# Narrow products of the norms' sums, router joins and rank columns widened to 96 moving columns

## The reference

```python
def ec_moe(h, w_router, w_gate, w_up, w_down):
    cap = EC_CAPACITY_FACTOR * n // N_EXPERTS
    aff = jax.nn.softmax(h.astype(jnp.float32) @ w_router.astype(jnp.float32), axis=-1)
    g, idx = lax.top_k(aff.swapaxes(1, 2), cap)
    xs = jax.vmap(lambda hb, ib: hb[ib])(h, idx)
    a = jax.nn.silu(jnp.einsum('becd,edf->becf', xs, w_gate)) * jnp.einsum('becd,edf->becf', xs, w_up)
    y = jnp.einsum('becf,efd->becd', a, w_down) * g[..., None].astype(h.dtype)
```

## Time and profile before

| | |
|---|---|
| median of 3 runs | 2208.03 us (2206.87 to 2209.65) |
| the profiled execution | 2207.79 us |
| its span | 2206.0 us |
| TensorE busy | 2164.8 us, 98% of the span |
| VectorE busy | 998.0 us, 45% |
| ScalarE busy | 375.3 us, 17% |
| mean granted clock of TensorE | 0.991 |
| DMA | 570.28 MB, mean 259 GB/s |

### The profile page before, as it was taken

The page is one execution under the profiler, slowest core; times in us unless marked ns, Lnnn a source line. Parts: engine busy times, 40 slices in busy tenths (PEclk is TensorE's granted clock), DMA queues, the critical chain, the costliest instruction groups (busy, mean ns, idle before and its releaser), DMA issues.

```text
span 2206.0 us, 25276 instructions
## 1 busy us (share of the span) xinstructions
PE 2164.8 (98%) x10282; PEld 1320.1 (60%) x10282; DVE 998.0 (45%) x1468; ACT 375.3 (17%) x743; POOL 78.8 (4%) x103
## 2 busy tenths in 40 slices
PE   7999999999999999999999999999999999999999
PEld 3443588888886777857444444437888744444443
DVE  2983397788845544832312222215555322222222
ACT  3003312002123112842100000002000300000000
POOL 1110100000021000001000000001000000000000
PEclk9999999999999999998999999999999899999999
DMA  9538244677641112032899999997112599999997
GB/s 348 193 97 297 77 153 153 234 257 282 212 179 39 39 53 77 1 153 115 367 428 429 428 430 428 428 426 261 68 77 81 242 411 428 428 429 429 428 429 310
DMA packets 110140, 570.28 MB, mean 259 GB/s; under 512 B 9929, under 2 KB 18670, under 8 KB 82414
## 3 DMA queue, kind: packets, MB, share of 16 engines
q1 hardware_dynamic: 107328, 564.55, 63.7%
q10 hardware_dynamic: 2734, 4.64, 0.9%
HBM read 561.06 MB, written 2.10 MB: 255 GB/s over the span
## 4 chain that ended last, share of the span: by engine, by line
PE 85%; DMA 9%; DVE 3%; ACT 1%; issue 1%; ACTq 0%; SPq 0%; POOL 0%; DVEq 0%
PE psum L1709 23%; PE psum L2210 18%; PE psum L2194 9%; PE psum L1440 6%; DMA ring<-in_moe_w_down_dram 5%; PE psum L2302 4%; PE psum L1857 4%; PE psum L2248 4%; PE psum L1881 3%; PE psum L2038 2%; DMA ring<-in_mlp_w_dram 2%; PE psum L2014 2%; PE psum L1989 2%; PE psum L1653 1%; DVE arena L2549 1%; PE psum L1603 1%
## 5 line engine op out<-in xcount | busy, mean ns | idle before, releaser
L2210 PE MATMUL psum<-ring,arena 128*64 128x512 f32 x2048 | 446.0, 594 | 3.6 <-DMA ring<-in_moe_w_up_dram 3.6
L2210 PEld LDWEIGHTS psum<-ring,arena 128*64 128x64 f32 x2048 | 144.3, 137 | 296.6 <-issue 284.7
L2194 PE MATMUL psum<-ring,arena 128*64 128x512 f32 x768 | 224.3, 594 | 1.7 <-DMA ring<-in_moe_w_down_dram 1.7
L3121 DVE TENSOR_TENSOR arena<-psum,arena 128x512 f32<-128x512 f32 x32 | 34.0, 1062 | 357.7 <-PE psum L2210 357.7
L1440 PE MATMUL psum<-hT,ring 128*128 128x512 f32 x416 | 181.9, 598 | 3.0 <-ACT hT L960 3.0
L1709 PE MATMUL psum<-ring 128*128 128x256 f32 x640 | 143.2, 380 | 3.4 <-DVE roots L2693 3.2
L1440 PEld LDWEIGHTS psum<-hT,ring 128*128 128x128 f32 x416 | 79.1, 191 | 103.1 <-issue 97.5
L1709 PE MATMUL psum<-hT,ring 128*128 128x256 f32 x608 | 135.9, 379 | 0.0
L1709 PEld LDWEIGHTS psum<-ring 128*128 128x128 f32 x640 | 120.9, 190 | 23.9 <-issue 7.8
L2248 PEld LDWEIGHTS psum<-arena 128*128 128x128 f32 x1024 | 118.4, 194 | 11.4 <-issue 11.4
L1709 PEld LDWEIGHTS psum<-hT,ring 128*128 128x128 f32 x608 | 115.3, 190 | 16.4 <-issue 0.8
(11 more groups left out here) (430 smaller groups left out, 2571.0 us busy)
## 6 DMA issues: line engine op xcount, KB each, us to landing
ring<-in_moe_w_gate_dram SPq DMA_DIRECT2D x64, 2048.0 KB, 19.0
ring<-in_moe_w_up_dram SPq DMA_DIRECT2D x64, 2048.0 KB, 16.1
ring<-in_moe_w_down_dram SPq DMA_DIRECT2D x44, 2048.0 KB, 18.9
ring<-in_ada_w_dram SPq DMA_DIRECT2D x24, 2048.0 KB, 8.1
ring<-in_mlp_w_dram SPq DMA_DIRECT2D x16, 2048.0 KB, 8.6
hT<-in_moe_w_down_dram SPq DMA_DIRECT2D x16, 2048.0 KB, 13.9
ring<-in_w_mod_dram SPq DMA_DIRECT2D x12, 2048.0 KB, 13.7
ring<-in_conv_w_in_dram SPq DMA_DIRECT2D x6, 2048.0 KB, 18.7
```

The costliest lines, as they stand in the source:

```text
L2194: ins = pe.matmul(psum[64 * e:64 * e + 64, bank + nh, :], src[:, 4 * h + k, 64 * e:64 * e + 64], w[:, k, nh * N:(nh + 1) * N], start=h == ...
L2210: ins = pe.matmul(psum[64 * nh:64 * nh + 64, bank + e, :], src[:, 4 * h + k, 64 * e:64 * e + 64], w[:, k, nh * N:(nh + 1) * N], start=h == ...
```

## The change

`COPIES = 96`. A view `copies(bank)` splits the first 4 x 96 columns of a bank into one run of 96 columns for each token group. Every narrow product now writes 96 columns: token sums and rank columns 96 times the same sum, joins six copies of the 16 logits, the x norm's sums 48 copies of the pair (and 48 columns with a stride of two where only one of the pair is made). The moving side is a wider slice of `ones_d`, or the old operand broadcast. Readers take the first copy. The rank columns of the second expert are written into bank 7 instead of bank 6. Number and order of the instructions and all waits stay as they were.

```diff
+        COPIES = 96
+        def copies(bank):
+            return psum[:, bank, 0:NT * COPIES].rearrange("p (t c) -> p t c", t=NT)
 ...
-                    ins = pe.matmul(psum[:, STAT, tt:tt + 1], src[:, tt * P:(tt + 1) * P], const("ones_d")[:, 0:1],
+                    ins = pe.matmul(copies(STAT)[:, tt, :], src[:, tt * P:(tt + 1) * P], const("ones_d")[:, 0:COPIES],
 ...
-                    at = psum[:, t % 6, tt * E:(tt + 1) * E]
+                    at = copies(t % 6)[:, tt, :].rearrange("p (c e) -> p c e", e=E)
+                    wide = [P, COPIES // E, E]
 ...
-                        ins = pe.matmul(at, tmp[:, 0, tt * P:(tt + 1) * P], const("stack")[:, 0:E], start=tt == 0,
+                        ins = pe.matmul(at, tmp[:, 0, tt * P:(tt + 1) * P],
+                                        const("stack")[:, 0:E].unsqueeze(1).to_broadcast(wide), start=tt == 0,
 ...
-                            ins = pe.matmul(at, xT[:, j, tt * P:(tt + 1) * P], rw_gain[:, layer, j, :],
+                            ins = pe.matmul(at, xT[:, j, tt * P:(tt + 1) * P],
+                                            rw_gain[:, layer, j, :].unsqueeze(1).to_broadcast(wide), ...
 ...
-                        ins = pe.matmul(at[:, w:w + 1], src[:, tt * P:(tt + 1) * P], const("ones_d")[:, 0:1],
+                        ins = pe.matmul(at[:, :, w], src[:, tt * P:(tt + 1) * P], const("ones_d")[:, 0:COPIES // 2],
 ...
-                        ins = pe.matmul(at, src[:, P * m:P * m + P], feature_w[:, tile, :], start=False, stop=last,
+                        ins = pe.matmul(at, src[:, P * m:P * m + P],
+                                        feature_w[:, tile, :].unsqueeze(1).to_broadcast([P, COPIES // 2, 2]), ...
 ...
-                            ins = pe.matmul(psum[:, BANK_WIDE[0], 2 * j + e:2 * j + e + 1], beats[e][m][:, P * j:P * j + P],
-                                            one[:, 0:1], start=m == j, stop=m == NT - 1, skip_group_check=True)
+                            ins = pe.matmul(copies(BANK_WIDE[e])[:, j, :], beats[e][m][:, P * j:P * j + P],
+                                            one[:, 0:1].to_broadcast([P, COPIES]), start=m == j, stop=m == NT - 1, skip_group_check=True)
 ...
-                        ins = pe.matmul(psum[:, STAT, at:at + 1], late_out[m][:, H * i + P * tt:H * i + P * tt + P],
-                                        const("ones_d")[:, 0:1], start=False, stop=True, skip_group_check=True)
+                        ins = pe.matmul(copies(STAT)[:, at, :], late_out[m][:, H * i + P * tt:H * i + P * tt + P],
+                                        const("ones_d")[:, 0:COPIES], start=False, stop=True, skip_group_check=True)
```

More of the change, by code:

```diff
@@ L945, in token_root @@
                     act.wait_ge(S["n_ms"], 1)
-                act.activation(n_tok[:, 0, :], psum[:, STAT, 0:NT], ACT.Sqrt, bias=eps[:, 0:1])\
+                act.activation(n_tok[:, 0, :], copies(STAT)[:, :, 0], ACT.Sqrt, bias=eps[:, 0:1])\
                     .then_inc(S["rms_ready"], 1)
@@ L1325, in softmax @@
                     act.wait_ge(S["sq_used"], DT * FFN0 + DT)
-                act.activation(tok[:, 0, :], psum[:, STAT, 0:NT], ACT.Sqrt, bias=eps[:, 0:1]).then_inc(S["rms_ready"], 1)
+                act.activation(tok[:, 0, :], copies(STAT)[:, :, 0], ACT.Sqrt, bias=eps[:, 0:1]).then_inc(S["rms_ready"], 1)
                 act.activation(tok[:, 2, 0:1], one[:, 0:1], ACT.Exp)
@@ L1551, in join_logits @@
                         for j in (() if layer and tt < 2 else (4, 5) if layer else (DT - 1,)):
-                            ins = pe.matmul(at, xT[:, j, tt * P:(tt + 1) * P], rw_gain[:, layer, j, :],
-                                            start=False, stop=j != 4, skip_group_check=True)
+                            ins = pe.matmul(at, xT[:, j, tt * P:(tt + 1) * P],
+                                            rw_gain[:, layer, j, :].unsqueeze(1).to_broadcast(wide), start=False, stop=j != 4, skip_group_check=True)
                 if part:
@@ L1559, in x_stat @@
                 for m, tt in enumerate(tts):
-                    at = psum[:, STAT, 2 * tt:2 * tt + 2]
+                    at = copies(STAT)[:, tt, :].rearrange("p (c w) -> p c w", w=2)
                     if tile is None:
-                        ins = pe.matmul(at[:, w:w + 1], src[:, tt * P:(tt + 1) * P], const("ones_d")[:, 0:1],
+                        ins = pe.matmul(at[:, :, w], src[:, tt * P:(tt + 1) * P], const("ones_d")[:, 0:COPIES // 2],
                                         start=w == 0 and m == 0, stop=False, skip_group_check=True)
                     else:
-                        ins = pe.matmul(at, src[:, P * m:P * m + P], feature_w[:, tile, :], start=False, stop=last,
+                        ins = pe.matmul(at, src[:, P * m:P * m + P],
+                                        feature_w[:, tile, :].unsqueeze(1).to_broadcast([P, COPIES // 2, 2]), start=False, stop=last,
                                         skip_group_check=True)
@@ L2775, in _ @@
                     w2_outputs(half, nh)
-            means = psum[:, STAT, 0:2 * NT].rearrange("p (t c) -> p c t", c=2)
+            means = copies(STAT)[:, :, 0:2].rearrange("p t c -> p c t")
             dve.wait_ge(S["x_ms"], 1)
@@ L3034, in wide @@
                     return ap.unsqueeze(2).to_broadcast([P, NT, E])
-                ps = psum[:, T_LG[layer] % 6, 0:NT * E].rearrange("p (a b) -> p a b", a=NT)
+                ps = copies(T_LG[layer] % 6)[:, :, 0:E]
                 dve.wait_ge(S["rms_ready"], ROUTED[layer] + 1)
@@ L3063, in route_all @@
                 link(dve.tensor_tensor(first_two, first_two,
-                                       psum[:, BANK_WIDE[0], 0:2 * NT].rearrange("p (t e) -> p t e", e=2), ALU.subtract))
+                                       psum[:, BANK_WIDE[0]:BANK_WIDE[1] + 1, 0:NT * COPIES]
+                                       .rearrange("p e (t c) -> p t e c", t=NT)[:, :, :, 0], ALU.subtract))
             def rounds(layer, rs):
```

## The result

The change makes the kernel faster: median 2197.95 us (2196.58 to 2200.86) against 2209.03 us (2206.87 to 2211.44), six runs each, a ratio of 0.995 with a 95% interval of 0.9939 to 0.9961. That is 11.1 us less, where 13 were forecast; 2197.95 lies just inside the forecast's own range of 2192 to 2198, at its upper end. The profiled execution took 2198.42 us with a span of 2196.6, against 2207.79 and 2206.0: 9.4 us less.

What follows compares the result with a forecast made beforehand. TensorE, slowed by 34.1 us at half clock, was taken to bound the kernel. Savings of 7.0 (layer 0), 5.0 (layer 1) and 1.0 (x norm), minus 0.1 for wider products, made 12.9 us: 2195 us, range 2192 to 2198.

Steps and rivals of the forecast that it cites:

- What sets the end, and the clock: TensorE sets the end nearly everywhere; its half-level clock, 34.1 us in both routes and x norm, would become full.
- Columns up to 128 are free: In the 248 widened records, spacing follows the clock alone, so 96 columns add only 0.1 us in all.
- Rival 4: Widened records: moving columns and weight loads don't overlap, 21 us added against 12.9 gained, 2216 us; chance 0.05.
- rival 2: Routes and x norm: copies don't feed the clock, stretches stay at 0.50, time about 2208 us; chance 0.07.
- Rival 3: Routes: transposes don't count as activity for the clock, so only 5.4 us is gained, 2202.4 us; chance 0.04.
- Layer 0, 7.0 us: Layer 0's route: with the full clock, the gather's second half starts at 1037.7 instead of 1044.66, saving 7.0 us.
- the affine turn: Layer 0's route: 32 small records, 1.39 us at half level, taken as between 0.7 and 1.39 at full.
- Layer 1, 5.0 us: Layer 1's route: the gather starts at 1730.05 instead of 1735.04, with waits of 0.9 and 0.45 us; 5.0 us saved.
- x norm, 1.0 us: The x norm's widening: eight records at full level end 0.8 to 1.0 us earlier; 1.0 us saved.
- Nothing is given back in the expert loops: Expert loops: an earlier gather frees ring slots earlier, so the DMA-bound stretch moves as a whole and all savings count.
- The sum: Whole kernel: 7.0 + 5.0 + 1.0 - 0.1 = 12.9 us saved, giving about 2195 us.
- Rival 1: Routes: the clock still falls in part at TensorE's new waits, giving 3.3 to 6.5 us back; chance 0.12.

Runs made afterwards that it cites:

- e1: The change's layout with the old 1, 2 and 16 moving columns, against the kernel before: median 2208.08 us against 2209.38, ratio 0.9997.
- e3: The change with only the rank columns put back to one column, against the kernel before: median 2202.21 us, ratio 0.9976.
- e2: The new layout with only the rank columns 96 wide, the other sums narrow, against the kernel before: median 2201.86 us, ratio 0.9973.
- e6: The change with 128 copies in place of 96: median 2197.99 us beside 2197.31 for the change on the same chip.

## Why the prediction was right, point by point

**What sets the end, and the clock.** Right. The half level stood where the narrow products were, and e1 to e3 move it with them. One of the forecast's two rows for a level that holds was luck, though: from 1506.4 to 1513.2 of the kernel before, one-column sums among spare products kept 1.00, but in e1 and e2 the same sums among the same spare products were followed by the half level, from 1512.7 and 1510.4. That mixture holds the level in some executions only. The gather of 128-column records was the sound half of the argument.

**Columns up to 128 are free.** Right, taken at 0.1 us. The median distance between starts is 0.112 us at full level with 1 column (L1467 before), 96 (L2125 after) and 128 (L2125 in e6). Rival 4 is refuted by e6, rival 2 by the first seven rows after and by e1.

**Transposes.** The Trainium skill says in "TensorE: Matmul & The Clock Gate", "Part 4: PE-mode transpose", that the full level does not engage for transposes; by that rule their stretches would have stayed at half level. The rows after, 1.00 from 1020.1 to 1030.3 with 24 transposes and the 8 of the widening in it, disagree, as the earlier trace rows did. Rival 3 is refuted.

**Layer 0, 7.0 us.** From the projections' end (L1521, now L1526, at 1018.22 and 1020.17) to the second half of the gather it is 20.08 us where it was 26.44: 6.4 us. The mis-sized term is the affine turn, put at 0.7 to 1.39 us, with the widening at a middle value. It took 1.38 us (1026.20 to 1027.58), as at half level, so the widening came 0.3 us later than forecast. Small excesses between the widening and the ranks (2.79 us, 2.7 forecast) and between the ranks and the first gather (5.80, 5.65 forecast) make most of the other 0.3 us. The wait ahead of the ranks was forecast as 0.5 and is 0.39; the one ahead of the gather, 0.25 in the forecast (1033.4 to 1033.65), is 0.23.

**Layer 1, 5.0 us.** From L1531 (1714.64, now L1536 at 1710.27) to the gather 15.61 us where it was 20.40: 4.8 us. Forecast waits 0.9 and 0.45, measured 0.87 and 0.39.

**x norm, 1.0 us.** 0.9 us.

**Nothing is given back in the expert loops.** Right: layer 0's gate products start 4.41 us earlier than before (1048.33 and 1043.92), and layer 1's joins behind the loops 4.31 us earlier (1717.88 and 1713.57). The last 460 us keep it as well: 9.2 us at layer 1's gate products (1742.74 and 1733.55), 9.4 at the end.

**The sum.** 6.4 + 4.8 + 0.9 = 12.1 us in the three places, 12.9 forecast. The step that a profile of before could not give is what happened outside them: in the execution profiled after, x norm's sums began 1.8 us later than before (674.56, 672.73), most of it around the half level from 190.6 (TensorE is 0.4 us ahead of the execution before at 191 and 1.0 us behind at 193; from there to the x norm's sums another 0.8 us was lost outside any fall), and another 1.0 us was lost between the x norm and the projections, where the fall at 869.9 is. 12.1 - 1.8 - 1.0 = 9.3, the 9.4 of the profiled pair. The medians, which mix executions with and without such falls, are 11.1, 12.0 and 8.8 us apart in the three comparisons of the change with before. Rival 1 (falls within the routes in spite of the new waits) did not happen in any of the seven profiles with 96 or 128 copies everywhere.

## What to carry to other kernels

Look at the granted clock beside the queue of TensorE before weighing a stretch of narrow products: where the moving side had a few columns behind full weights, float32 as here, its width up to the weights' 128 cost nothing that showed, and what the clock loses is paid by whatever stands behind it too. When work gets faster, read off which chain is now the next one, and move into each wait only what it holds: a filler is cover for one wait and can't be spent twice. In a kernel that waits at a few places, one profile holds a sample of the clock's falls; take the sum of an edit from the stretches that it touches, and the noise from several profiles.

## What had not been expected of the hardware

The 32 small records of the affine turn (32 weight columns, 8 moving) took 1.39 us at half level and 1.38 us at full; their spacing, 0.043 us, does not follow the clock, while that of the records with 128 weights does (0.213 and 0.112 us). The level can fall while TensorE is never kept waiting: ahead of the falls in the routes the narrow records followed each other at 0.111 us, as closely as wide ones do, and yet only where 96 or 128 columns moved was the level held there in every profile.
